# Retention's query projection among the head transposes, and block 2's feed-forward norm and router tile by tile in its output projection

## The reference

```python
# block 1
rq = split_heads(h @ w_in[:, retention's query columns])       # 512 x 512, no norm
gk = l2norm(...); gq = l2norm(...) * 128 ** -0.5               # the delta rule's keys and queries
rq, rk = apply_rope(rq, cos, sin), apply_rope(rk, cos, sin)
# block 2
x  = x + g1 * (concat([y_conv, y_attn]) @ w_out)               # output projection
h2 = rms_norm(x, norm_ffn_g) * (1 + sc2) + sh2                 # feed-forward norm
aff = softmax(h2 @ w_router)                                   # 512 x 16
wts, tok = top_k(aff.T, 64)                                    # each expert takes its 64 best tokens
x  = x + g2 * scatter(experts(h2[tok]) * wts)
```

## Time and profile before

| what | value |
|---|---|
| three runs, median (lowest to highest) | 3336.83 us (3332.36 to 3341.05) |
| the profiled execution, its own time | 3329.19 us |
| its span, first to last instruction | 3327.3 us |
| PE busy | 2872.6 us, 86% |
| DVE, POOL, ACT busy | 978.4, 610.6, 458.0 us |
| mean granted TensorE clock | 0.943 of full speed |

### The profile page before, as it was taken

How to read it: one execution, slowest core, us unless ns; L and a number is a source line. 1 busy time by engine, 2 the same in 40 slices (tenths; PEclk the granted TensorE clock), 3 DMA queues, 4 the chain that set the end, 5 groups by cost and what they waited for, 6 DMA issues and landing times.

```text
span 3327.3 us, 34278 instructions
## 1 busy us (share of the span) xinstructions
PE 2872.6 (86%) x14021; PEld 1437.2 (43%) x14021; DVE 978.4 (29%) x1607; ACT 458.0 (14%) x957; POOL 610.6 (18%) x433
## 2 busy tenths in 40 slices
PE   4998599998998989997999779678688988888887
PEld 2644567775443545443544333344222222222232
DVE  2041645554113351111111258662212111121122
ACT  2011222221101211111111111341000000000000
POOL 1001255642200114342434210311000000000000
PEclk7999799999998999998999989887899999999999
DMA  5010044332322349997999721123799999999997
GB/s 224 27 63 14 23 140 130 118 121 86 114 76 92 143 183 373 384 369 275 370 377 359 275 98 51 41 106 130 282 421 420 420 421 420 421 420 421 421 420 291
DMA packets 127475, 793.24 MB, mean 238 GB/s; under 512 B 21954, under 2 KB 22338, under 8 KB 56920
## 3 DMA queue, kind: packets, MB, share of 16 engines
q1 hardware_dynamic: 102616, 744.32, 55.8%
q0 software_dynamic: 22880, 37.81, 4.7%
q10 hardware_dynamic: 1824, 8.91, 0.7%
HBM read 769.37 MB, written 38.86 MB: 243 GB/s over the span
## 4 chain that ended last, share of the span: by engine, by line
PE 61%; DMA 23%; DVE 9%; issue 3%; ACT 2%; POOL 1%; SPq 0%; POOLq 0%; ACTq 0%; DVEq 0%
DMA arena<-in_w_down 12%; PE b L2853 10%; PE b L1795 6%; DMA yd<-arena 6%; PE b L1359 5%; PE b L474 3%; PE b L476 3%; PE b L1809 3%; PE b L2888 2%; DMA arena<-h2d,arena 2%; PE b L2375 2%; PE b L615 2%; PE b L1047 2%; PE b L1060 2%; PE b L1423 2%
## 5 line engine op out<-in xcount | busy, mean ns | idle before, releaser
L2853 PE MATMUL b<-arena 128*64 128x512 f32 x2048 | 456.5, 601 | 23.2 <-DMA arena<-in_w_up 10.1
L1795 PE MATMUL b<-arena 128*64 128x256 f32 x3072 | 355.1, 383 | 3.0 <-DMA arena<-in_w_gu 1.8
L2868 PE MATMUL b<-arena 128*64 128x512 f32 x1024 | 245.1, 603 | 60.7 <-DMA arena<-in_w_down 60.6
L2853 PEld LDWEIGHTS b<-arena 128*64 128x64 f32 x2048 | 153.7, 137 | 320.3 <-issue 262.8
L1795 PEld LDWEIGHTS b<-arena 128*64 128x64 f32 x3072 | 212.8, 137 | 114.2 <-issue 4.1
L2113 POOL DMA_INDIRECT yd<-arena x96 | 152.5, 1588 | 354.1 <-ACT arena L1896 163.5
L1809 PE MATMUL b<-arena 128*64 128x512 f32 x768 | 186.0, 604 | 1.0 <-issue 0.9
L2068 DVE TENSOR_TENSOR arena<-arena,b 128x128 f32<-128x128 f32 x96 | 27.8, 290 | 515.6 <-ACT arena L1886 478.1
L1359 PE MATMUL b<-arena 128*128 128x512 f32 x384 | 166.8, 596 | 9.6 <-DMA arena<-in_w_in 9.6
L2868 PEld LDWEIGHTS b<-arena 128*64 128x64 f32 x1024 | 64.5, 135 | 240.7 <-DMA arena<-in_w_down 141.0
L2964 DVE TENSOR_TENSOR arena<-arena,b 128x512 f32<-128x512 f32 x32 | 20.6, 686 | 467.7 <-PE b L2853 467.7
(11 more groups left out here) (469 smaller groups left out, 3707.3 us busy)
## 6 DMA issues: line engine op xcount, KB each, us to landing
arena<-in_w_gu SPq DMA_DIRECT2D x65, 2048.0 KB, 10.3
arena<-in_w_gate SPq DMA_DIRECT2D x128, 1024.0 KB, 27.0
arena<-in_w_up SPq DMA_DIRECT2D x128, 1024.0 KB, 26.1
arena<-in_w_down SPq DMA_DIRECT2D x128, 1024.0 KB, 25.3
arena<-in_w_dn SPq DMA_DIRECT2D x65, 1024.0 KB, 13.2
arena<-in_w_mod SPq DMA_DIRECT2D x80, 512.0 KB, 3.8
arena<-in_w_in SPq DMA_DIRECT2D x19, 2048.0 KB, 8.5
arena<-yd SPq DMA_DIRECT2D x12, 512.0 KB, 7.9
```

Source lines behind the costliest of these rows:

```text
L1795: x = e.matmul(ps[i % 2][64 * j:64 * j + 64, 0:256], XGT[i % 2][:, k % 4, (k // 4) * 64:(k // 4) * 64 + 64], GUB[place_of(w)][:, k, j * 25 ...
L2853: x = e.matmul(ps[b + c][64 * hf:64 * hf + 64, :], XS[q % 2][:, kb, (n % 2) * 64:(n % 2) * 64 + 64], w[:, u * 512:(u + 1) * 512], start=(k ...
L2868: x = e.matmul(ps[4][64 * hf:64 * hf + 64, :], H[:, c * 4 + j, hi * 64:hi * 64 + 64], w[:, i * 1024 + hf * 512:i * 1024 + hf * 512 + 512], ...
```

## The change

1. The queries' four groups leave `projections` and stand in `by_heads`, behind the 16 groups of transposes and ahead of the ten that turn keys and queries back. Their weights stay in slot `wr[0]`, loaded as before. ACT copies all four out. The embedding of the queries, on DVE and on POOL, now waits for the last of these copies.
2. In block 2 the norm and the router move into `mixer_out2`. PE transposes tile t-1 behind the last group of tile t, and routes tile t-2 behind the first group of tile t; three pieces are left for the end. ACT squares each tile when DVE has added it to `x`, and DVE scales it. The output projection uses three PSUM banks in turn (5, 6, 7), the transposes banks 0 to 3, the logits bank 4.
3. The router's weights are loaded ahead of the first expert pieces; the logits are read from PSUM by DVE, and ACT no longer copies them. The ring still has 13 slots; some lie elsewhere.

```diff
@@ projections
-    for ci, (kind, M, tiles) in enumerate((("rk", RK, 6), ("rv", RV, 6), ("rq", RQ, 4)), 4):
+    for ci, (kind, M, tiles) in enumerate((("rk", RK, 6), ("rv", RV, 6)), 4):
...
+    K.wrq, K.came_wrq = wr[0], came_w[0]
@@ by_heads
+    groups += [("rq", t) for t in range(4)]
     groups += [("kt", t) for t in range(6)] + [("qt", t) for t in range(4)]
...
+    on_act = lambda i: i % 2 == 0 or groups[i][0] == "rq"
+    by = lambda i: act_ if on_act(i) else dve
...
+            if kind == "rq":
+                if t == 0:
+                    e.wait_ge(*K.came_wrq.at(6))
+                for k in range(8):
+                    x = e.matmul(p[:, :], K.HT[:, k, hs(t)], K.wrq[:, k, :], start=(k == 0), stop=(k == 7))
+                x.then_inc(*mm.up(i))
+                continue
...
+            if i == N_TM + 3:
+                e.wait_ge(*act_.at("out", N_TM + 3))
                 K.rope_q.dve(e)
...
+        e.wait_ge(*act_.at("out", N_TM + 3))
         K.rope_q.pool(e)
@@ mixer_out2
+    def bank(g):
+        return g[1] if g[0] == "yct" else 5 + (2 * g[1] + g[2]) % 3
...
+            if i >= 7:
+                e.wait_ge(*dve.at(*groups[i - 3]))
...
+            if g[0] == "o" and g[1]:
+                if g[2]:
+                    norm.transpose(e, g[1] - 1)
+                elif g[1] > 1:
+                    route(e, g[1] - 2)
+        route(e, 2)
+        norm.transpose(e, 3)
+        route(e, 3)
+
+    def route(e, t):
+        norm.out(e, t)
+        if t == 0:
+            e.wait_ge(*K.came_wr2.at())
+        for k in range(8):
+            x = e.matmul(ps[4][:, t * 16:t * 16 + 16], H2T[:, k, hs(t)], wrt[:, k, :], start=(k == 0), stop=(k == 7))
+        x.then_inc(*route_mm.up("route", t))
...
+        for t in range(4):
+            e.wait_ge(*dve.at("x", t, 1))
+            norm.square(e, t)
+            if t:
+                norm.out_act(e, t - 1)
+        norm.out_act(e, 3)
...
             e.tensor_tensor(X[:, t, cs], X[:, t, cs], otmp[c], ALU.add).then_inc(*dve.up("x", t, c))
+            if c:
+                norm.scale(e, t)
+                if t:
+                    norm.out_dve(e, t - 1)
+        norm.out_dve(e, 3)
+
+    def pool(e):
+        all_of(e, *K.att)
+        norm.shifts(e)
@@ experts2
     def sp(e):
         all_of(e, *K.att)
+        e.dma_start(K.wrt2, I["w_rt_2"].rearrange("p k n -> p (k n)")).then_inc(*K.came_wr2.up())
...
-        norm.transposes(e)
-        norm.done(e)
-        e.wait_ge(*came_wr.at())
-        for t in range(4):
-            for k in range(8):
-                x = e.matmul(ps[t][:, 0:16], H2T[:, k, hs(t)], wrt[:, k, :], start=(k == 0), stop=(k == 7))
-            x.then_inc(*mm.up("route", t))
         e.wait_ge(*dve.at("aff"))
...
-        e.tensor_reduce(m4, EXf, AX, ALU.max).then_inc(*dve.up("top"))
+        logits = ps[4][:, 0:64].rearrange("p (t n) -> p t n", t=4)
+        e.wait_ge(*mm.at("route", 3))
+        e.tensor_reduce(m4, logits, AX, ALU.max).then_inc(*dve.up("top"))
```

More of the change, by code:

```diff
@@ L674, in target @@
         kind, t = groups[i]
+        if kind == "rq":
+            return K.RQ[:, t, :], ps[i % 7][:, :]
         if kind in dst:
@@ L709, in dve_ @@
                 l2(e, "q", GQ, 4, rq)
+            if i == N_TM + 3:
+                e.wait_ge(*act_.at("out", N_TM + 3))
                 K.rope_q.dve(e)
-            if i % 2 == 1:
+            if not on_act(i):
                 o, s = target(i)
@@ L2652, in mixer_out2 @@
     otmp = [lsc[:, 0:512], lsc[:, 512:1024]]
+    under = K.area(K.keep1 + 16504)
+    K.H2Tf, K.H2a, K.wrt2 = under(4096), under(2048), under(128)
+    K.after2 = under.at
+    K.H2b = K.arena[:, K.keep1 + 8192:K.keep1 + 10240]
+    K.H2 = [K.H2a[:, 0:1024], K.H2a[:, 1024:2048], K.H2b[:, 0:1024], K.H2b[:, 1024:2048]]
+    H2T, wrt = K.H2Tf.rearrange("p (k n) -> p k n", k=8), K.wrt2.rearrange("p (k n) -> p k n", k=8)
+    K.came_wr2 = S.dma("wrt2")
     mm, dve, act_ = S("out2_mm"), S("out2_dve"), S("out2_act")
+    route_mm = S("ec_mm")
     K.mix2 = (mm, dve, act_)
+    K.norm_f = norm = Norm(K, "ffn2", [(X[:, t, :], K.A2, K.S2, t * 128) for t in range(4)], K.H2, lsc[:, 1024:2048],
+                           K.ss2[:, 8:12], H2T, range(4))
     groups = [("yct", t) for t in range(4)] + [("o", t, c) for t in range(4) for c in range(2)]
-    def evacuated(e, g):
-        e.wait_ge(*(act_ if g[0] == "yct" and g[1] % 2 == 0 else dve).at(*g))
+    def bank(g):
+        return g[1] if g[0] == "yct" else 5 + (2 * g[1] + g[2]) % 3
     def pe(e):
@@ L2662, in pe @@
         for i, g in enumerate(groups):
-            p = ps[i % 8]
-            if i >= 8:
-                evacuated(e, groups[i - 8])
+            p = ps[bank(g)]
+            if i >= 7:
+                e.wait_ge(*dve.at(*groups[i - 3]))
             if g[0] == "yct":
@@ L2693, in dve_ @@
         K.rows_b2.done(e)
-        for i, g in enumerate(groups[4:], 4):
+        for g in groups[4:]:
             _, t, c = g
@@ L2741, in experts2 @@
     mm, dve, act_, pool_ = S("ec_mm"), S("ec_dve"), S("ec_act"), S("ec_pool")
-    norm = Norm(K, "ffn2", [(X[:, t, :], K.A2, K.S2, t * 128) for t in range(4)], [H2[:, t, :] for t in range(4)], XG[0], ss2[:, 8:12], H2T, range(8))
+    norm = K.norm_f
     pieces = []
@@ L2790, in pe @@
         opened(e)
[L2791 to L2797 removed]
         e.wait_ge(*dve.at("aff"))
         for t in range(4):
[L2800 removed]
+            x = e.transpose(ps[5][0:16, hs(t)], AF[:, t, :], K.ident)
         x.then_inc(*mm.up("affT"))
@@ L2891, in act @@
         opened(e)
-        norm.run_act(e, lambda e, i: None)
-        for t in range(4):
-            e.wait_ge(*mm.at("route", t))
-            e.activation(EXf[:, t, :], ps[t][:, 0:16], ACT.Copy).then_inc(*act_.up("logit", t))
         e.wait_ge(*dve.at("shifted"))
@@ L3002, in pool @@
         opened(e)
-        norm.shifts(e)
         e.wait_ge(*norm.pool.at("ffn2", 3))
```

32 lines of the change are left out of this document (12 added, 20 removed).

## The result

| | before | after |
|---|---|---|
| median of four runs (lowest to highest) | 3338.22 us (3332.36 to 3341.05) | 3298.94 us (3289.99 to 3307.14) |
| the profiled execution | 3329.19 us | 3299.59 us |
| its span | 3327.3 us | 3297.8 us |
| PE busy | 2872.6 us | 2877.6 us |
| DVE, POOL, ACT busy | 978.4, 610.6, 458.0 us | 976.1, 612.0, 456.7 us |

A forecast was written before the change was run, and what follows sets the result against it. Bound by the chain of waits (PE 61%, transfers 23%), then by weights once the first expert starts. Gains of 17.6 in block 1 and 15.7 in block 2 make 33.3 us: from median 3336.8 to 3303.5, range 3290 to 3314.

The forecast's parts named there:

- Part 1: Block 1: the queries' projection on PE hides both norms, so retention starts at 335.5; gain 17.6 us (17.3 to 22.1).
- the row of the keys' embedding: Block 1: the queries' embedding takes 9.25 us, as the keys' did, since both halves now start together.
- the 4.75 us of the queries before: Block 1: lower bound for the queries' embedding, DVE's half before, when POOL's half was done under the scaling.
- Part 2: Block 2: norm and router move into the output projection, exponential at 2312.05 not 2327.77; gain 15.7 us (10.6 to 19.9).
- now ACT is idle for 3 us and loads the table there: Block 2's tail: the exponential's table load of 1.28 us lies in ACT's idle time, ahead of the exponential.
- The term of 0.5 us behind the last router: Block 2's tail: estimate for DVE's maximum and subtraction between the last router and the exponential, 0.5 us.
- The sum: Whole kernel: 17.6 + 15.7 = 33.3 us gained, from the median 3336.8 to 3303.5; chance 0.83.
- the bound stretch starts when the first expert starts: Block 2: the weight stream stands still 34.7 us until the first expert's matmuls free a slot, so an earlier start counts.
- The weights hid nothing: Rival, block 2: the first expert starts earlier but its weights do not, leaving only block 1's gain: 3319.2; chance 0.05.
- The queries were not held back: Rival, block 1: a bank or copy holds PE until the roots are done, losing that block's gain: 3321.1; chance 0.04.
- The clock did not fall in either place of the change: Rival: narrow work drops the clock to 0.50; block 2 alone 3336, chance 0.04; both blocks 3363.6, chance 0.04.
- the rule quoted there: Skill's rule that transposes do not count as busy PE; taken to speak for the falling clock, against the trace.

The follow-up runs named there:

- the parts alone: The kernel before with only one move each: the queries' projection, 3319.40 us (ratio 0.9961); block 2's norm and router, 3315.46 us (0.9946).
- the versions built on after: The changed kernel with further edits (embedding on DVE, early table load, added matmuls, router work fourfold, combinations): 3289.16 to 3319.55 us.
- part 2 alone: The kernel before with only block 2's feed-forward norm and router moved, block 1 as before: 3315.46 us, ratio 0.9946.
- the first set alone: The changed kernel with five unused wide matmuls on PE ahead of block 2's router of tile 2 only: one run, 3301.69 us.

## Why the prediction was right

**Part 1: forecast 17.6 us, measured 17.1** (17.6 without the 0.5 us by which the projections before it ran later in this execution). Step by step: the projection ended 27.5 us behind the transposes, as worked out from 64 records. The norms ended 21.0 us after POOL's start, 6 us ahead of the projection (said: some 5). PE did not wait between the queries' groups. The embedding began 0.8 us behind the projection (0.7), took 9.2 us (9.25, the row of the keys' embedding, which started its halves together in the same way), and retention followed 3.5 us later (3.4). That the row of the keys was the right one, and not the 4.75 us of the queries before, has a reason that the prediction did not know: the two engines exclude each other, as the embedding on DVE alone showed. The norms were 1.7 us shorter than forecast (22.7), and the trace points the same way: DVE's small operation ahead of the queries' scaling took 1.90 us before and ended at 342.66, when POOL's half of the embedding ended (342.63); it takes 0.17 now that POOL is idle there.

**Part 2: forecast 15.7 us, measured 14.8** in the first pair. The inserts cost 5.3 us (60.5 instead of 55.2; said 5.7) at a clock of 1.00. Behind the projection the router of tile 2 began at +5.2 (+5.4), the transposes of tile 3 at +8.7 (+8.85), the last router at +11.5 (+11.65) and ended at +15.05 (+15.1), at 1.2 GHz. The step that failed is the last one, "now ACT is idle for 3 us and loads the table there": ACT was idle for 5.4 us and loaded nothing, the load came behind DVE's subtraction and put 1.3 us on the path. The term of 0.5 us behind the last router measured 2.0 (2298.30 to 2300.31). The step took the place of the load from the kernel before, where it did lie ahead of the wait; it did not carry over. Moving the load brought the tail to 15.4, next to the 15.65 that the step had worked out (its terms add up to 15.6).

**The sum.** Steps of 17.1 to 17.6 and 14.8 give about 32 us, forecast 33.3; the medians gave 39.3, 34.0 and 34.5. That 33.3 lies so close to the last two is in part luck: the parts alone gave 13.5 and 17.5 where their steps give 17.1 and 14.8, and the runs of one kernel spread by 8 to 17 us. The first profiles alone gave 29.6, since after lost 4.2 us in block 1's router to the clock. The stretch from the first expert to the end, bound by the weights, was forecast to stay as it is: it took 969.7 and 969.4 us in the profiles of before, 967.7, 967.9 and 966.7 in those of after, and 966.9 to 970.8 in the versions built on after. Some 2 us may thus have come from there; why was not tried. That the bound stretch starts when the first expert starts, on which the gain of part 2 rested, held: SP's standstill moved as a whole.

**The rivals.** The weights hid nothing (part 2 alone gained 17.5 us). The queries were not held back. The clock did not fall in either place of the change; the rule quoted there from the Trainium skill ("TensorE: Matmul & The Clock Gate", Part 4: PE-mode transpose), that transposes do not count as a busy PE, decided nothing here, where they stood among wide matmuls. But the rival's mechanism was shown with four times the narrow work, so its chance was rightly not nothing.

## What to carry to other kernels

Before an order is changed, look for the engine that will wait next: here DVE's 7 us under the projection and ACT's 5 us ahead of the exponential were both visible places for work that lay open behind. An engine's idle time hides only what may be issued in it. A table load can stand behind the waits of its activation, as here, or ahead of them, as in the kernel before, and the trace of the one place does not tell for the other; a small activation of the same function ahead of the last wait moved the load here. Narrow matmuls went well here in sets of 16 records between wide ones; 64 in a row lost the full clock, and then the first wide work behind them ran at the lower one too.

## What the runs showed that was not expected

- Splitting the rotary embedding over DVE and POOL cost time: 9.2 us on both, 6.8 us on DVE alone.
- The clock in a stretch of narrow matmuls is not the same in every execution of one program: block 1's router ran in 7.33 us in one profile of before and in 11.55 in the other. What decides between the two was not tried.
- The clock can be bought: matmuls without use, placed where PE waits, made the two routers behind the projection 1.93 and 1.85 us long instead of 3.57 each (the first of the two took 2.80 to 3.57 in the three profiles of the changed kernel). With the first set alone the clock held for 16 narrow records and eight transposes and was gone for the next 16.
- The place of a table load can change with the code around it: the exponential's load lay ahead of its wait in the kernel before and behind it in the changed one, where all of its 1.3 us lay on the path.
